# Second layer's attention: split values stationary, normalised split weights of two query blocks moving

## The reference, cut to what matters

```
cq, ckv, k_rope, gate = split(u @ w_in, [256, 384, 416])
q  = rmsnorm(cq)  @ w_uq      # 16 heads x 96, the last 32 rotated
kv = rmsnorm(ckv) @ w_ukv     # 16 heads x (64 k, 64 v); k_rope rotated, shared
s  = (q_nope.k_nope + q_rope.k_rope) * 96**-0.5     # 1024 x 1024 per head
p  = softmax(s);  o = p @ v                          # per block of 128 queries
y  = o * silu(gate);  out = y @ w_out
```

## Time and profile before

| | us |
|---|---|
| median of 3 runs (4585.83 to 4594.2) | 4586.41 |
| the profiled execution, its device time | 4581.67 |
| its span (first to last instruction) | 4579.9 |
| PE busy in the span | 4337.8 (95%) |
| DVE / ACT / POOL busy | 1856.7 / 1277.5 / 1281.5 |
| mean granted TensorE clock | 0.935 of full |
| heads stage, first piece to first matmul of `pe_out` | 1179.30 to 1803.89 |

### The profile page before, as it was taken

One profiled execution on the slowest core, in us unless ns is written; L12 is line 12 of the kernel. 1 busy time (PEld: TensorE's weight loads), 2 busy tenths in 40 slices (PEclk: granted clock), 3 DMA queues, 4 the chain that ended last, 5 costly groups with the idle time before them and its releaser, 6 DMA issues.

```text
span 4579.9 us, 51693 instructions
## 1 busy us (share of the span) xinstructions
PE 4337.8 (95%) x20631; PEld 3531.6 (77%) x20631; DVE 1856.7 (41%) x3427; ACT 1277.5 (28%) x2692; POOL 1281.5 (28%) x1225
## 2 busy tenths in 40 slices
PE   8999999798999999899888999999999888999998
PEld 4969788477899998787556888887786566888887
DVE  2020210455355554612754343334514734333434
ACT  1120211213344443312543322112313533312222
POOL 1403120145100000632123444334332042433431
PEclk9959689699999999999988999999998998999999
DMA  5101012422100000310013111112210022111112
GB/s 184 54 23 42 23 37 70 145 96 69 41 7 8 8 8 28 104 48 23 1 44 102 46 56 47 47 46 70 97 43 13 1 67 98 48 47 44 56 49 97
DMA packets 224513, 244.67 MB, mean 53 GB/s; under 512 B 43848, under 2 KB 165208, under 8 KB 224272
## 3 DMA queue, kind: packets, MB, share of 16 engines
q1 hardware_dynamic: 190432, 162.78, 12.0%
q10 hardware_dynamic: 33840, 78.58, 4.9%
HBM read 209.10 MB, written 30.07 MB: 52 GB/s over the span
## 4 chain that ended last, share of the span: by engine, by line
PE 84%; DVE 9%; ACT 3%; issue 1%; DMA 1%; POOL 1%; SPq 0%; ACTq 0%; DVEq 0%; POOLq 0%
PE ps L127 79%; PE ps L130 5%; DVE tlo L139 1%; DVE cst_sm L150 1%; DVE tfi L147 1%; ACT m_junk L133 0%; POOL mix_z L139 0%; DVE m_hb L147 0%; ACT f_ta L133 0%; DVE m_z L147 0%; ACT thi L133 0%; DVE gt_yr L139 0%; DVE m_z L139 0%; DVE c_rn L139 0%; DVE tfl L147 0%
## 5 line engine op out<-in xcount | busy, mean ns | idle before, releaser
L136 POOL CAST whi<-wst 128x512 fp32r<-128x512 f32 (+3 forms) x562 | 389.9, 694 | 2767.0 <-DMA wst<-in_a_w_in 561.2
L139 POOL TENSOR_TENSOR wlo<-wst,whi 128x512 fp32r<-128x512 f32 (+3 forms) x562 | 733.7, 1306 | 45.0
L127 PE MATMUL ps<-thi,whi 128*128 128x512 f32 x1760 | 692.2, 393 | 14.0 <-ACT m_z L133 5.6
L127 PE MATMUL ps<-tlo,whi 128*128 128x512 f32 x1760 | 690.5, 392 | 0.0
L127 PE MATMUL ps<-thi,wlo 128*128 128x512 f32 x1760 | 689.8, 392 | 0.0
L127 PE MATMUL ps<-whi,thi 128*128 128x512 f32 (+3 forms) x1752 | 670.1, 382 | 3.5 <-DVE mix_z L139 2.6
L127 PE MATMUL ps<-wlo,thi 128*128 128x512 f32 (+3 forms) x1752 | 665.3, 380 | 0.0
L127 PE MATMUL ps<-whi,tlo 128*128 128x512 f32 (+3 forms) x1752 | 664.9, 379 | 0.0
L147 DVE SCALAR_TENSOR_TENSOR f_ta<-f_ua,tfi,f_ta 128x1024 f32<-128x1024 f32 x88 | 120.6, 1371 | 736.7 <-ACT f_ta L133 735.1
L127 PEld LDWEIGHTS ps<-whi,thi 128*128 128x128 f32 x1752 | 370.5, 211 | 50.7 <-DVE mix_z L139 3.0
L127 PEld LDWEIGHTS ps<-whi,tlo 128*128 128x128 f32 x1752 | 370.1, 211 | 47.3
(11 more groups left out here) (266 smaller groups left out, 6145.0 us busy)
## 6 DMA issues: line engine op xcount, KB each, us to landing
wst<-in_w_up SPq DMA_DIRECT2D x704, 64.0 KB, 2.0
wst<-in_ada_w SPq DMA_DIRECT2D x96, 256.0 KB, 3.6
wst<-in_w_down SPq DMA_DIRECT2D x88, 256.0 KB, 2.6
wst<-in_a_w_in SPq DMA_DIRECT2D x96, 192.0 KB, 2.4
wst<-in_w_in SPq DMA_DIRECT2D x64, 256.0 KB, 2.7
wst<-in_w_out SPq DMA_DIRECT2D x32, 256.0 KB, 4.6
m_xr<-scr_x ACTq DMA_DIRECT2D x16, 512.0 KB, 3.6
scr_x<-m_z ACTq DMA_DIRECT2D x16, 512.0 KB, 2.7
```

Of the source, the lines that this page charges most:

```text
L127: return self.none if self.e is None else self.e.matmul(*a, **k)
L136: return self.none if self.e is None else self.e.tensor_copy(*a)
L139: return self.none if self.e is None else self.e.tensor_tensor(*a)
```

## The change

Scores, exponentials and transposes keep their shapes. The rest of the heads stage becomes:

- POOL multiplies the exponentials by the reciprocal of the row sum, 128x1024 in place, before PE transposes them (`b_unit`); DVE takes the reciprocal one turn earlier. The scale 96^-0.5 goes into the table `k_qtab`, so the maximum is negated inside the `tensor_reduce` and the `tensor_scalar` is gone.
- Both transposed banks are split: ACT writes hi (`pth`), DVE subtracts to lo (`ptl`). The two buffers of each hold a pair of query blocks (256 columns).
- Values are split into 64 hi and 64 lo columns of one stationary block. Per pair p of units (turns i = 2p+5), 16 matmuls of 256 moving columns replace 2 x 8 fp32 products. Hi and lo rows of the result lie on two partition halves; ACT copies one to SBUF and DVE adds the other.
- Output and gate are kept transposed (features on partitions): the gate projection is made transposed, its 8 DMAs and the 16 groups of transposes at the end go. POOL multiplies output by gate (64x256 per pair). At the end ACT and DVE split the result in 16 pieces (`Y_ORDER`), and `pe_out` waits for it block by block (`kready`).
- POOL also splits q pieces (one `qs` buffer in place of two), and splits the weights at fixed turns of its loop. v pieces move to turns 6 and 7 of a head, and the piece comes after the product on PE.

```diff
@@ pool_heads (new loop) @@
+        for i in range(128 + 7):
+            if i and self.piece_at(i - 1):
+                self.pool_piece_lo(q, *self.piece_at(i - 1))
+            if i % 8 == 0 and i < 112:
+                self.split(q, ("head", i // 8 + 2))
+            if i % 8 == 4 and 40 <= i < 128:
+                n = i // 8 - 5
+                self.split(q, ("wo", "b", n // 8, n % 8))
+            if 1 <= i < 129:
+                u = i - 1
+                q.wait_ge(*S.at("b_rec", u))
+                q.tensor_scalar(self.bp[u % 3], self.bp[u % 3], self.bstat(u, 2), None, ALU.mult).then_inc(*S.up("b_unit", u))
+            if i >= 6 and i % 2 == 0 and i < 134:
+                p = (i - 6) // 2
+                y, o = self.head_out(p)
+                q.wait_ge(*S.at("evac_v", ("bo", p)))
...
+                q.tensor_tensor(y, o, y, ALU.mult).then_inc(*S.up("b_y", p))
@@ pe_heads @@
-                                 [S.at("exp", ("b", i - 2))])
+                                 [S.at("b_unit", i - 2)])
+            if i >= 5 and i % 2 == 1:
+                p = (i - 5) // 2
...
+                    for k in range(4):
+                        v = self.bv[h % 3][n][:, k, :]
+                        q.matmul(ps[:, b, 0:256], v, self.pth[x][n][:, k, :], start=(n == 0 and k == 0), stop=False)
+                        ins = q.matmul(ps[:, b, 0:256], v, self.ptl[x][n][:, k, :], start=False, stop=(n == 1 and k == 3))
@@ act_heads @@
             if 2 <= i < 130:
                 u = i - 2
+                if u >= 4:
+                    q.wait_ge(*S.at("pv", ("b", u // 2 - 2)))
+                for n in range(2):
+                    key = ("bt", u, n)
+                    q.wait_ge(*S.at("turned", key))
+                    q.activation(self.pth[u // 2 % 2][n][:, :, u % 2 * 128:u % 2 * 128 + 128],
+                                 ps[:, B.of(key), :].rearrange("p (a b) -> p a b", a=4), ACT.Copy).then_inc(*S.up("hi", key))
+            if i >= 5 and i % 2 == 1:
+                p = (i - 5) // 2
+                r, o = 64 * (1 - p // 4 % 2), self.head_out(p)[1]
+                q.wait_ge(*S.at("pv", ("b", p)))
...
+                q.activation(o, ps[r:r + 64, B.of(("bo", p)), 0:256], ACT.Copy).then_inc(*S.up("b_half", p))
@@ dve_heads @@
-                q.wait_ge(*S.last("v_seq"))
-                q.tensor_scalar(self.bstat(i, 1), self.bstat(i, 0), -scale, None, ALU.mult).then_inc(*S.up("b_max", i))
+                q.tensor_reduce(self.bstat(i, 0), ps[:, b:b + 2, :].rearrange("p a b -> p (a b)"), AXX, ALU.max,
+                                negate=True).then_inc(*S.up("b_max", i))
+            if 1 <= i < 129:
+                u = i - 1
+                q.wait_ge(*S.at("exp", ("b", u)))
+                q.reciprocal(self.bstat(u, 2), self.bstat(u, 1)).then_inc(*S.up("b_rec", u))
             if 2 <= i < 130:
                 u = i - 2
+                for n in range(2):
+                    key, r = ("bt", u, n), slice(u % 2 * 128, u % 2 * 128 + 128)
+                    q.wait_ge(*S.at("hi", key))
+                    q.tensor_tensor(self.ptl[u // 2 % 2][n][:, :, r], ps[:, B.of(key), :].rearrange("p (a b) -> p a b", a=4),
+                                    self.pth[u // 2 % 2][n][:, :, r].bitcast(F32), ALU.subtract).then_inc(*B.free(key, "evac_v"))
+            if i >= 5 and i % 2 == 1:
...
+                q.tensor_tensor(o, ps[r:r + 64, B.of(("bo", p)), 0:256], o, ALU.add).then_inc(*B.free(("bo", p), "evac_v"))
```

More of the change, by code:

```diff
@@ L1456, in act_latent, with gate_T @@
         for h in range(2):
[L1457 to L1460, removed]
+            for hf in range(2):
+                for m in range(4):
+                    key = (("bg", h), (m, hf))
                     q.wait_ge(*S.at("tile", key))
[L1462 to L1470, removed]
+                    if h != hf:
+                        q.wait_ge(*S.at("turned", ("lt", 4 * h + m)))
+                    q.activation(self.gate_T(4 * h + m, hf), ps[:, B.of(key), :], ACT.Silu).then_inc(*B.free(key, "evac_a"))
+                if h == 0 and hf == 0:
                     for j in range(4, 8):
                         out(j)
+    def gate_T(self, m, hf):
+        if m < 4:
+            return self.gx[:, m if hf else 8 + m, :]
+        return self.tfl[:, m, 0:512] if hf else self.gx[:, m, :]
     def dve_latent(self, q):
@@ L1617, in dve_piece @@
             q.wait_ge(*S.at("ld_qtab"))
-            if h:
-                q.wait_ge(*S.at("hi", ("piece", h - 1, what, hf)))
-            q.tensor_tensor(self.qs[hf][:], p, self.msh[:, r], ALU.mult).then_inc(*B.free(key, "evac_v"))
+            if (h, hf) != (0, 0):
+                q.wait_ge(*S.at("hi", ("piece", h if hf else h - 1, what, 1 - hf)))
+                q.wait_ge(*S.at("lo_p", ("hq", h if hf else h - 1, 1 - hf)))
+            q.tensor_tensor(self.qs[:], p, self.msh[:, r], ALU.mult).then_inc(*B.free(key, "evac_v"))
         elif what == "k":
@@ L1665, in pe_heads @@
                     q.wait_ge(*event)
[L1666 to L1677, removed]
+                for n in range(2):
+                    q.wait_ge(*B.done(("bt", 2 * p + 1, n)))
+                    q.wait_ge(*B.done(("piece", h // 2 * 2, "v", n)))
+                    for k in range(4):
+                        v = self.bv[h % 3][n][:, k, :]
+                        q.matmul(ps[:, b, 0:256], v, self.pth[x][n][:, k, :], start=(n == 0 and k == 0), stop=False)
+                        ins = q.matmul(ps[:, b, 0:256], v, self.ptl[x][n][:, k, :], start=False, stop=(n == 1 and k == 3))
+                ins.then_inc(*S.up("pv", ("b", p)))
+            if self.piece_at(i):
+                self.pe_piece(q, *self.piece_at(i))
     def bstat(self, i, n, w=1):
         return self.sm[:, 192 + i % 8 * 4 + n:192 + i % 8 * 4 + n + w]
+    Y_ORDER = [(0, 0), (1, 0), (2, 0), (3, 0), (4, 1), (4, 0), (5, 1), (5, 0), (6, 1), (6, 0), (7, 1), (7, 0),
+               (0, 1), (1, 1), (2, 1), (3, 1)]
     def act_heads(self, q):
         S, B, ps = self.S, self.B, self.ps
[L1684 to L1689, removed]
+        for piece in self.first_pieces():
+            self.act_piece(q, *piece)
+        for i in range(128 + 4):
             if i < 128:
@@ L1711, in dve_heads @@
+            if self.piece_at(i):
+                self.act_piece(q, *self.piece_at(i))
+        for kt, hf in self.Y_ORDER:
+            q.wait_ge(*S.at("b_y", 4 * (2 * kt + 1) + 2 * hf + 1))
+            q.wait_ge(*S.at("qk", ("b", 127)) if kt < 2 else S.at("turned", ("bt", 127, 1)) if kt < 4 else S.at("pv", ("b", 63)))
+            q.activation(self.thi[:, kt, half(hf)], self.gate_T(kt, hf), ACT.Copy).then_inc(*S.up("hi", ("by", kt, hf)))
     def dve_heads(self, q):
         S, B, ps = self.S, self.B, self.ps
-        scale = 96.0 ** -0.5
@@ L1714, in dve_heads @@
[L1714 to L1724, removed]
+        for p in self.first_pieces():
+            self.dve_piece(q, *p)
+        for i in range(128 + 4):
             if i < 128:
@@ new lines, in dve_heads @@
+            if i >= 5 and i % 2 == 1:
+                p = (i - 5) // 2
+                r, o = 64 * (p // 4 % 2), self.head_out(p)[1]
+                q.wait_ge(*S.at("b_half", p))
+                q.tensor_tensor(o, ps[r:r + 64, B.of(("bo", p)), 0:256], o, ALU.add).then_inc(*B.free(("bo", p), "evac_v"))
+            if self.piece_at(i):
+                self.dve_piece(q, *self.piece_at(i))
+        for kt, hf in self.Y_ORDER:
+            q.wait_ge(*S.at("hi", ("by", kt, hf)))
+            if kt >= 4 and hf == 0:
+                q.wait_ge(*S.at("lo", ("by", kt, 1)))
+            q.tensor_tensor(self.tlo[:, kt, half(hf)], self.gate_T(kt, hf), self.thi[:, kt, half(hf)].bitcast(F32),
+                            ALU.subtract).then_inc(*S.up("lo", ("by", kt, hf)))
```

155 lines of the change are left out of this document (80 added, 75 removed).

## The result

The changed kernel is slower. Its median is 4625.57 us (four runs, 4619.59 to 4635.42) against 4586.53 for the kernel before (four runs); the ratio is 1.0083, 95% interval 1.0062 to 1.0105, some 39 us. The forecast was 4585 with a range to 4606, so the time lies outside the range. The profiled execution took 4622.41 us with a span of 4620.6 and a mean granted clock of 0.926; before it was 4581.67, 4579.9 and 0.935.

The account below looks back on a forecast made before the run. PE, without idle time, was taken to bound the kernel; after the change a closed ring of DVE and ACT waits would. Ring +10.3, start -3.7 and end -7.8 gave -1.2 us, a median of 4585 us, range 4574 to 4606.

Parts of the forecast that it names:

- The reading of before: Heads stage of the old kernel: PE has no idle time and sets the turn, 4.04 us per unit plus 0.61 for pieces.
- the price of PE's work: Heads stage after the change: PE needs 3.91 us per unit, 0.74 less, worth 94 us if PE stays the bound.
- The ring: Heads stage: maximum, exponential, hi, two subtractions, next maximum wait in a closed loop, 4.20 us a turn; +10.3 us in all.
- the first two steps: Start of the maxima: the first two turns have no subtractions, so the third maximum comes 4.0 us after the first.
- The start: Start of the heads stage: the first maximum comes at about 1189.1 for 1192.76, -3.7 us.
- POOL: ... I take the copy's side, 1.1: POOL's multiplication in the heads stage, without a measured row: priced at 1.1 us between ends of 1.03 and 3.03.
- the forecast's threshold: Heads stage: POOL's multiplication is hidden up to 2.8 us, as 5.96 plus its time must fit in 8.74 per pair.
- the rival that it falls: PE's clock drops in gaps of the heads stage: +9 us at 0.87, +51 (4636) at 0.75; chance 0.05.
- The end: Last maximum to the first matmul of the output projection: 12.6 us for 20.4, -7.8 us.
- Nothing changes after the heads: Stages behind the heads stage: their time stays the same, no term in the sum.
- the stalls: Rival: small stalls where pieces, halves and banks meet, 0.1 us a turn, +12.5 us, 4597; chance 0.10.
- M = 3.03: Rival: POOL's multiplication takes 3.03 us and sets the turn in the heads stage, +17 us, 4602; chance 0.12.

Follow-up runs that it names:

- experiment 4: Changed kernel with POOL multiplying only 128 of 1024 columns and ACT making hi of unit i-2 before the exponential of unit i; 4474.65 us, ratio 0.9744.
- experiment 5: Changed kernel with POOL multiplying only 128 of 1024 columns and six useless matmuls in PE's gaps; 4592.88 us, ratio 1.0009 to the kernel before.
- experiment 1: Changed kernel with POOL multiplying only 128 of the 1024 columns, the rest left unnormalised; 4600.69 us, ratio 1.001 to the kernel before.
- experiment 2: Changed kernel with POOL multiplying only 512 of the 1024 columns, the rest left unnormalised; 4611.45 us, ratio 1.0038 to the kernel before.
- experiment 3: Changed kernel, full multiplication, with six useless matmuls before PE's transposes in odd turns after a turn without a piece; 4599.45 us, ratio 1.0008.
- experiment 7: Changed kernel with ACT's hi before the exponential, DVE normalising columns 0 to 511 and POOL 512 to 1023; 4510.31 us, ratio 0.9826.

## Why the prediction was wrong

**The reading of before and the price of PE's work: right.** PE without a gap was the bound; 3.91 us per unit after were forecast, and experiment 4 with PE full shows 3.84 (9 us less over the 127 steps).

**The ring: right.** 4.17 measured for 4.20 forecast in the bare turn. With the clock kept up and POOL short (experiment 5) the maxima take 599.7 for 601. Its terms hold one by one: 1.24 (1.27), 1.10 (1.11), 0.62 (0.63), 1.21 (1.20). That the total is so near is partly luck: the first two steps take 6.3 us in the kernel after and in all eight experiments, for the 4.0 forecast, and 125 turns at 0.03 less give 3.8 back.

**The start: right, with luck in the decimals.** 1188.92 for 1189.1. The kernels of experiments 1, 2, 3 and 5, which differ from it only in the stage's loop, have the first maximum anywhere from 1187.96 to 1191.87.

**"POOL: ... I take the copy's side, 1.1": wrong, it is 2.845.** I had the ends 1.03 and 3.03, and chose by the number of tensor inputs; the true value lies at the other end. The Trainium skill, "GPSIMD Engine Reference", section 3.1, gave an estimate of 0.9 us for a body with one input; here the measurement decides, at three times as much. Taken for itself this miss costs about what the forecast's threshold says: 5.96 + 2.845 = 8.81 for 8.74 in a pair, 4 us in all, and with the clock held up (experiments 3 and 5) it measured 605.5 - 599.7 = 5.8 us, 0.1 per pair. One us of this is a single low stretch that experiment 3 still has in head 0.

**The clock: the step that failed.** The sum took PE's work at full clock throughout, and the rival that it falls got 0.05, with the argument "Against: PE streams more columns per us than now". The runs show the clock falling in a stage where PE is busy 85%, and that is worth 27.3 us, the largest of the unforecast terms. The prediction had what it needed to ask: it expected gaps of up to 1.8 us, and the earlier trace rows stood beside them, where a stretch with gaps had 0.87. The way it priced the rival failed too. It spread a mean clock evenly over PE's longest way and got +9 us at 0.87 and +51 at 0.75; the measured mean is 0.95, milder than either, and costs 27.3. The loss isn't spread: nearly all of it falls on 19 turns, at half clock, on the way that sets the turn, and each of them pays about 1.4 us.

Not every gap is followed by a fall. Between the first and the last maximum PE has 25 gaps of 2.0 us or more; behind 20 of them the granted clock goes to 0.50, behind five it stays at 1.00. One of the five, in the timeline and the windows of the kernel after:

```profile
1486.97 1.06 PE L130 MATMUL ps<-cst_ident,tfi 128*128 128x128 f32 x8 [2.29 <-POOL tfi L142]
```

```profile
1487.00:1491.00 4.00, 4.00 (x30) 3.78 (x31) 2.28 (x5) 2.56 (x5) 3.54 (x2) 1.00 0.00 0
```

The kernel before has one such gap, in its first turns, and its clock stayed at 1.00 as well:

```profile
1203.90 1.09 PE L130 MATMUL ps<-cst_ident,tfi 128*128 128x128 f32 x8 [2.58 <-ACT tfl L133]
```

What decides between the two is not shown by any run. The sum from the runs:

| part of first to last maximum | us | from |
|---|---|---|
| ring, pieces, additions at full clock | 599.7 | experiment 5 |
| POOL's longer multiplication at full clock | +5.8 | 3 less 5 |
| the clock | +27.3 | after less 3 |
| after | 632.8 | |

Of the clock's part 15.4 us are there with POOL's multiplication short (615.1 - 599.7, experiments 1 and 5), so the ring's own gaps bring it on; the rest comes as POOL gives PE more gaps of 2 us and over (25 for 16 in experiment 1). The two wrong steps are thus not independent: M near the forecast's "hidden up to 2.8" is nearly hidden from the ring, but not from PE's idle time.

**The end: wrong, from the same terms.** 18.9 us for 12.6; kernels with a short multiplication measured 13.2 (experiments 1 and 5). The last of POOL's multiplications stands open there, and the low clock, as little is left to overlap with them; the one before it lies behind a product at half speed. PE's timeline at the end of the kernel after shows both, a wait for POOL and transposes at half speed:

```profile
1830.63 1.94 PE L130 MATMUL ps<-cst_ident,tfl 128*128 128x128 f32 x8 [3.27 <-POOL tfl L142]
```

**Nothing changes after the heads: nearly.** For 320 us behind the stage the windows of both kernels agree within 0.1 us of PE's busy time. The 4.0 us come later, in stages that the change doesn't touch; five of the eight experiments have 2.9 to 4.1 of them too. One stretch there has a lower clock (0.85 from 3440.56 to 3760.56 after, 0.89 from 3403.89 to 3723.89 before); why it does is open.

**The range** names the stalls and M = 3.03 as its high end, both as additions at full clock. Its own terms, +17 and +12.5 on 4585, give 4614 and not 4606, and neither reaches 4625.57: the cases that share one cause (longer waits, then a slower engine behind each) were never added up.

## What to carry to other kernels

Before work is taken off the engine that is the bound, follow the new order through all in-order engines and look for a closed ring; if it is longer than what is left on that engine, the gain is gone, and swapping two instructions in one of them can give it back, once nothing else is as long (here 112 us with POOL's multiplication short, but 28.6 with it whole). When PE turns from bound to waiting, ask what its clock will do, and price a fall as half speed in the turns that it hits, not as a mean over the stage and not at nothing: here 20 of 25 gaps of 2 us and over had one behind them, at about 1.4 us each. An operation that moves to POOL and has no row should be priced at the dear end of its neighbours, or measured first.

## What the runs showed of the hardware

- POOL's `tensor_scalar` with a per-partition scalar, fp32 in SBUF: 0.603 us for 128 columns (experiment 1), 1.564 for 512 (experiment 2), 2.845 for 1024 (after): 0.28 us and 2.5 ns per column. DVE's for 512 columns took 0.49 in 98 of the 128 turns of experiment 7; the mean of 0.61 holds the other 30.
- In these 30 DVE's multiplication started while POOL was subtracting a q piece (1.3 us), and took 1.02 us on average: it was held until POOL's instruction was through. The other way round POOL's 512 columns took 1.81 for 1.564 where they started beside DVE's 0.49. The Trainium skill, "SBUF — State Buffer", section "Who interferes with whom", has DVE and GpSimd share a pair of ports that one of them can lock for the whole of an instruction. The trace agrees with it where DVE comes second; where POOL comes second it loses 0.24 us, about half of DVE's 0.49. Experiment 7, one row pair of each kind:

```profile
1396.60 1.30 POOL L139 TENSOR_TENSOR tlo<-ml_qs,thi 128x512 fp32r<-128x512 f32 x1 [0.29 <-ACT thi L133]
...
1397.15 1.03 DVE L142 TENSOR_SCALAR tfi<-tfi,cst_sm 128x512 f32<-128x512 f32 x1
...
1402.02 0.49 DVE L142 TENSOR_SCALAR tfi<-tfi,cst_sm 128x512 f32<-128x512 f32 x1
1402.08 1.85 POOL L142 TENSOR_SCALAR tfi<-tfi,cst_sm 128x512 f32<-128x512 f32 x1 [0.55 <-DVE cst_sm L156]
```

- Six matmuls without use in PE's gaps (experiment 3) took the profiled execution from 4622.41 to 4596.67 us, and the ratio to before from 1.0083 to 1.0008.
